# A chunked scan whose C Bᵀ products move forward in the order, a weighting done in one pass, and MLP products spread over four banks

## The reference, cut to what matters

```
cb      = C Bᵀ                              # 128 x 128 for each group
y_diag  = (cb * mask * decay * dt) x        # decay: 128 x 128 for each head
y_off   = (C h_prev) * exp(acs)
h       = chunk_decay * h_prev + Bᵀ(decay_to_end * dt * x)
y       = y_forward + y_backward + d_skip * x;   then y * SiLU(z)
```

## Time and profile before

| | us |
|---|---|
| median of 3 runs | 1688.41 (1687.32 to 1689.16) |
| profiled execution, its own time | 1688.6 |
| its span, first to last instruction | 1686.7 |
| PE busy | 1592.4 (94% of the span) |
| DVE busy | 1020.2 (60%) |
| ACT busy | 653.8 (39%) |

### The profile page before, as it was taken

How to read it: one execution, slowest core, us unless ns; L and a number is a source line. 1 busy time by engine, 2 the same in 40 slices (tenths; PEclk the granted TensorE clock), 3 DMA queues, 4 the chain that set the end, 5 groups by cost and what they waited for, 6 DMA issues and landing times.

```text
span 1686.7 us, 27239 instructions
## 1 busy us (share of the span) xinstructions
PE 1592.4 (94%) x11141; PEld 1503.7 (89%) x11141; DVE 1020.2 (60%) x1429; ACT 653.8 (39%) x1133; POOL 99.0 (6%) x155
## 2 busy tenths in 40 slices
PE   6999999989997998888899999999999999999997
PEld 2899999989997988888755699999989999999997
DVE  5777677738663677887566453436863353343468
ACT  3544444424463256675455533323521121121220
POOL 1001022100101100000000001000000000000000
PEclk9999999989998999999899999999999999999999
DMA  9545455432677666686440164335112222223221
GB/s 320 158 146 182 155 183 184 149 118 86 211 240 248 204 220 212 189 277 202 156 160 26 50 204 145 129 127 181 51 51 75 76 75 76 77 75 101 62 89 63
DMA packets 159895, 241.63 MB, mean 143 GB/s; under 512 B 8064, under 2 KB 126576, under 8 KB 156720
## 3 DMA queue, kind: packets, MB, share of 16 engines
q1 hardware_dynamic: 136608, 171.45, 31.2%
q0 software_dynamic: 12304, 47.72, 7.7%
q10 hardware_dynamic: 10880, 20.97, 4.6%
HBM read 195.06 MB, written 45.06 MB: 142 GB/s over the span
## 4 chain that ended last, share of the span: by engine, by line
PE 79%; DVE 10%; ACT 5%; issue 2%; DMA 2%; SPq 1%; ACTq 0%; DVEq 0%
PE acc L842 62%; PE tp L842 14%; ACT arena L1716 2%; PE tp L1257 1%; ACT whi L1472 1%; DVE arena L2272 1%; DVE wlo L1987 1%; PE tp L950 1%; DMA arena<-in_x_sample 1%; DVE arena L2274 1%; DMA y_nat<-arena 1%; DVE st L2005 1%; DMA raw<-in_w_in 1%; ACT whi L1853 1%; DVE wlo L2451 1%
## 5 line engine op out<-in xcount | busy, mean ns | idle before, releaser
L842 PE MATMUL acc<-hh,whi 128*128 128x322 f32 x1152 | 299.6, 321 | 13.3 <-issue 4.1
L842 PE MATMUL acc<-hl,whi 128*128 128x322 f32 x1152 | 294.5, 317 | 0.0
L842 PE MATMUL acc<-hh,wlo 128*128 128x322 f32 x1152 | 293.2, 315 | 0.0
L1987 DVE TENSOR_TENSOR wlo<-raw,whi 128x2048 fp32r<-128x2048 f32 x74 | 169.5, 2290 | 95.3 <-ACT whi L1472 95.3
L842 PEld LDWEIGHTS acc<-hh,whi 128*128 128x128 f32 x1152 | 204.6, 194 | 15.7 <-issue 4.5
L1472 ACT ACTIVATE whi<-raw 128x2048 fp32r<-128x2048 f32 x74 | 141.1, 1907 | 171.0 <-PE acc L842 166.9
L842 PEld LDWEIGHTS acc<-hl,whi 128*128 128x128 f32 x1152 | 205.9, 194 | 0.0
L842 PEld LDWEIGHTS acc<-hh,wlo 128*128 128x128 f32 x1152 | 205.7, 194 | 0.0
L842 PE MATMUL acc<-whi,hh 128*128 128x256 f32 x640 | 183.8, 287 | 0.0
L842 PE MATMUL acc<-whi,hl 128*128 128x256 f32 x640 | 180.6, 282 | 0.0
L842 PE MATMUL acc<-wlo,hh 128*128 128x256 f32 x640 | 180.4, 282 | 0.0
(11 more groups left out here) (296 smaller groups left out, 2909.8 us busy)
## 6 DMA issues: line engine op xcount, KB each, us to landing
raw<-in_w_in SPq DMA_DIRECT2D x38, 1024.0 KB, 6.9
raw<-in_w_mlp SPq DMA_DIRECT2D x32, 1024.0 KB, 5.4
arena<-in_w_mod SPq DMA_DIRECT2D x24, 1024.0 KB, 6.2
arena<-decay_sums_t ACTq DMA_DIRECT2D x40, 512.0 KB, 5.5
arena<-xs_nat SPq DMA_DIRECT2D x8, 1024.0 KB, 8.1
raw<-in_w_ssd_o SPq DMA_DIRECT2D x8, 1024.0 KB, 6.2
y_nat<-arena POOLq DMA_DIRECT2D x6, 1024.0 KB, 7.2
arena<-y_nat SPq DMA_DIRECT2D x6, 1024.0 KB, 6.5
```

The costliest lines, as they stand in the source:

```text
L842: return pe.matmul(out, l, r, start=first, stop=last)
L1987: dve.tensor_tensor(wlo[:, slot], raw[:, slot], whi[:, slot].bitcast(F32), ALU.subtract).then_inc(lo["sem"], step(lo))
```

## The change

It has five parts.

1. Preparation: five of the six filling pieces (before: two) stand ahead of `turn_h0(1)` on PE, and so on ACT ahead of `h0_out`; one (before: four) stands behind.
2. Latent chunks: PE's `products` stands behind the chunk's first piece; before it stood behind all three. ACT starts `exps` of group 0 ahead of the chunk's first piece, no longer behind it. On DVE, only in chunk 1, `masked` and `weighted(0)` stand ahead of two of its three first pieces.
3. `weighted` is one multiplication of 1024 columns instead of two of 512, and the addition as before.
4. `gated` of the quads 0 and 1 stands behind `weighted(4)` and `weighted(6)`, and that of quad 2 behind the last `combined`.
5. The MLP's second products go through the four banks acc 0 to 3.

```diff
@@ PE, preparation and scan
-            fill(2)
+            fill(F_H0 - 1)
             pe.wait_ge(s["h0_in"], 32)
...
             turn_h0(1)
-            fill(F_H0 - 2)
+            fill(1)
...
             for c in range(1, NT):
-                fill(F_LAT[c - 1])
+                fill(1)
                 if c == 1:
                     pe.wait_ge(bfree["sem"], value(bfree))
                     pe.wait_ge(h0c["sem"], value(h0c))
                 b = (c + 1) % 2
                 products(b)
+                fill(F_LAT[c - 1] - 1)
                 pe.wait_ge(bnin[b]["sem"], due(bnin[b]))
@@ PE, second_products
-                first_two([acc[:, 0, 0:BW], acc[:, 2, 0:BW]], (2, 2))
+
+                first_two([acc[:, 0, 0:BW], acc[:, 1, 0:BW]], (4, 4))
...
                         step(free)
-                        pe.wait_ge(free["sem"], value(free, 2))
-                        mlp_products(acc[:, 2 * ((NT * b + t) % 2), 0:BW], t, whi[:, b % 2], wlo[:, b % 2],
+                        pe.wait_ge(free["sem"], value(free, 4))
+                        mlp_products(acc[:, (NT * b + t) % 4, 0:BW], t, whi[:, b % 2], wlo[:, b % 2],
@@ ACT
-            weights(2)
+            weights(F_H0 - 1)
...
             h0_out(backs[0])
-            weights(F_H0 - 2)
+            weights(1)
...
             for c in range(1, NT):
+                exps(NG * c)
                 weights(1)
-                exps(NG * c)
                 if c > 1:
                     squares(c - 1, 2, zq[:, 0])
+                exps(NG * c + 1)
                 weights(1)
-                exps(NG * c + 1)
@@ DVE, weighted
-                for d in range(2):
-                    last = dve.tensor_tensor(ee[:, b, d], ee[:, b, d], cbm[:, d, g].unsqueeze(1).broadcast_to([P, R, P]), ALU.mult)
-                do(last)
+                do(dve.tensor_tensor(ee[:, b], ee[:, b], cbm[:, :, g].unsqueeze(2).broadcast_to([P, 2, R, P]), ALU.mult))
@@ DVE, a latent chunk
                 if c == 1:
-                    weights(F_LAT[c - 1])
+                    weights(1)
                 masked()
                 for g in range(NG):
                     weighted(g)
-                    weights(F_LAT_G[g] + (F_LAT[c - 1] if g == 0 and c > 1 else 0))
+                    if g in (4, 6):
+                        gated(c, g // 2 - 2)
+                    weights(F_LAT_G[g] + (F_LAT[c - 1] - (c == 1) if g == 0 else 0))
...
                         if q:
                             combined(y, q - 1, y[:, 8 * q - 8:8 * q])
-                            gated(c, q - 1)
                 combined(y, 3, y[:, 24:32])
+                gated(c, 2)
                 gated(c, 3)
@@ DVE, second_round
-                        dve.tensor_tensor(xo[:, t, cols], xo[:, t, cols], acc[:, 2 * ((NT * b + t) % 2), 0:BW],
+                        dve.tensor_tensor(xo[:, t, cols], xo[:, t, cols], acc[:, (NT * b + t) % 4, 0:BW],
```

## The result

The changed kernel takes 1691.67 us (median of 20 runs, 1687.49 to 1698.47); the kernel before takes 1688.45 us beside it (20 runs, 1684.01 to 1691.05). The ratio is 1.0021, with a 95% interval of 1.0011 to 1.0031: slower, by 3.2 to 3.6 us where 9.5 were forecast. The profiled execution took 1695.16 us (span 1693.2), that is 6.6 us over the profiled one of before and 3.5 us over its own kernel's median.

A forecast was written before the change was run, and what follows sets the result against it. PE, busy 94% of the span, was taken to bound the kernel, and the change to move its waits: 27.0 − 3.0 − 8.6 − 1.4 − 4.5 = +9.5 us on 1688.6, forecast 1698 us, range 1690 to 1704 (own case 1694 to 1703).

The forecast's parts named there:

- The mechanism: Three chunk turns: C Bᵀ waits 6.1 us for DVE's last `combined`, half clock follows, group 1's wait stays; 9.0 us each.
- the bank is free in time: Rival at the turns: DVE finishes its last `combined` before PE's one piece, turns cost 0; 1671 us, chance 0.05.
- the wait ahead of group 1 goes away: Rival at the turns: early C Bᵀ removes group 1's wait, a turn costs 2.9 us; 1679.6 us, chance 0.03.
- transfers in the preparation: Rival: a z block's store queues behind the backward state's, taking back up to 8.6 us; 1702 to 1707 us, chance 0.06.
- the clock recovers sooner or falls less often: Rival: new stalls lose 1.7 us or nothing, or shorter waits keep the clock up; 1690 to 1692 us, chance 0.08.
- The savings: Forecast gains: preparation 8.6 us, chunk 1 1.4 us, inside four chunks 3.0 us, MLP 4.5 us.
- the clock term of the sum: Behind the new wait at each of three turns: 5.8 us at half clock lose 2.9 us.
- the rest inside the chunks: Four chunks: one `gated` pass fewer ahead of `weighted(6)` and one-pass weighting shorten PE's waits, saving 3.0 us.
- MLP and all else behind the scan: MLP's second products: four banks remove three PE waits of 1.5 us for DVE's adds, saving 4.5 us.
- its terms: Part 2: three turns cost 27.0 us; earlier products start group 1 of chunk 1 sooner, saving 1.4 us.
- the bounds of the clock and of the merged pass: Half-clock loss of 1.7 us, or none, instead of 2.9 us a turn; merged weighting pass between 1.08 and 1.29 us.

The follow-up runs named there:

- e2: The changed kernel with C Bᵀ of chunks 2 to 4 behind two of the three first pieces instead of one: 1681.57 us, ratio 0.9966.
- e5: The changed kernel with part 2 taken back on PE, ACT and DVE, the rest of the change kept: 1672.71 us, ratio 0.9906.
- e3: The kernel before with PE's C Bᵀ behind the first piece and nothing else of the change: 1718.57 us, ratio 1.0178.
- e6: The kernel before with part 1, the preparation, alone: 1680.53 us, ratio 0.9958.
- e9: e5 with ACT's order of the change, while C Bᵀ stays behind three pieces: 1683.90 us, ratio 0.9974.
- e4: The changed kernel with 54 matmuls whose output nobody reads ahead of C Bᵀ in chunks 2 to 4: 1686.48 us, ratio 0.9992.
- e1: The changed kernel with C Bᵀ behind all three first pieces again, on PE alone: 1693.41 us, ratio 1.0027.
- e12: The kernel before with parts 3 and 4 alone, the one-pass weighting and the later gating: 1683.11 us, ratio 0.9979.
- e11: e8 with the filling piece of group 4 moved ahead of group 3: 1666.31 us, ratio 0.9872 against the kernel before.
- e8: e5 with `weighted(1)` ahead of the lower splits in chunks 1 to 4: 1664.81 us, ratio 0.9875 against the kernel before.

## Why the prediction was right in its sign and wrong in its size

**The mechanism held.** PE stands 6.3 us at each of three turns (6.1 forecast), the clock falls behind it, and group 1's wait stays. From the end of group 7 (705.80 + 0.83 = 706.63 in PE's timeline) to group 1 a turn takes 738.41 − 706.63 = 31.8 us, against 733.47 − 710.75 = 22.7 in the earlier trace rows: 9.1 us more where 9.0 were forecast. e2 shows that the wait is lack of cover and e5 that part 2 alone makes the change slower. The rivals "the bank is free in time", "the wait ahead of group 1 goes away" and "transfers in the preparation" fall with these rows. The remaining one, "the clock recovers sooner or falls less often", had a chance of 0.08 and the time that came (1690 to 1692 us). It has half of the mechanism: the new stalls did lose what I gave them, the old waits ahead of group 1 lost less.

**The savings held**: parts 1, 5 and 3 with 4 each by themselves, above. The wait of the preparation went, the store had landed; chunk 1's group 1 came at 608.17 instead of 618.26, 10.1 us sooner, 10.0 forecast (8.6 + 1.4).

**The step that failed is the clock term of the sum**: 2.9 us of new loss for each turn, 8.7 in three, with the loss behind the four waits ahead of group 1 left as it was. The length of the half clock behind a wait is not fixed by that wait. These are the times of the same 32 matmuls behind the waits ahead of group 1, from the chains (us; a dash where they are not on the chain):

| kernel | chunk 1 | 2 | 3 | 4 |
|---|---|---|---|---|
| before | 7.01 | 7.25 | 7.40 | 7.44 |
| changed | 6.27 | 6.27 | 6.29 | 6.29 |
| e2 | 6.28 | 7.44 | 7.83 | 7.66 |
| e3 | 6.83 | 7.70 | 7.59 | 7.57 |
| e6 | 6.77 | 6.28 | – | 6.87 |
| e9 | 6.24 | 7.37 | 6.25 | 7.49 |

```profile
750.84 7.59 PE acc L842 x32
667.27 6.28 PE acc L842 x32
```

The first row is e3's, some 21 us behind a new stall of 6.9 us: nothing is given back. The second is e6's, without any new stall and behind the same wait of 3.16 us as in the kernel before (7.25): 1.0 us is given back. So the changed kernel's gain behind group 1 is real in its profile, but it is not shown to come from the new stalls.

In the profiled executions the whole account is: preparation −8.8, chunk 1 −1.3, turns +27.2, behind the four waits ahead of group 1 −4.0, the rest inside the chunks −3.0 (−3.0 forecast), MLP and all else behind the scan −3.6 (−4.5 forecast, see the last section). That is +6.5, as from span to span. Of the 3.0 us that this is under the forecast, the 4.0 behind group 1 are more than all; the MLP takes 0.9 back.

**The other 3 us** lie between the profiled execution and the median. The profiled execution of the changed kernel is 3.5 us over its median, that of before 0.2 us over its own. Executions of one kernel differ by their mean granted clock: of the changed kernel 1687.49 us came with 0.981, 1695.16 with 0.974, 1698.47 with 0.973. I made the sum against one execution and took each of its half-clock stretches as owed. Which stretch the median execution lacks stays open, since only one execution of each kernel was profiled. But in medians, too, the miss lies in part 2 and not in the savings: part 2 costs 19.4 us, where its terms were 27.0 − 1.4 = 25.6. The stalls of 18.9 us less 1.4 are 17.5 of those 19.4, so the clock's part is 1.9 us (3.8 either way) where 8.7 were forecast. e4 has it at 5 us (2.4 either way), e3, where PE's order alone was changed, at 9.3 (3.0 either way). The price of the clock is thus anything from next to nothing to the full 8.7, by what else stands in the kernel.

In the stretch from 500 to 870 us, 48 us stand at half clock before (PEclk 0.95 over the first 100 us, 0.93 over the other 270) and 49 us after (1.00 and 0.91), within 3 us of rounding. The sum had 8.7 us of new loss against 2.0 us given back in the preparation, 6.7 net, which would be over 13 us more at half clock. The advice of the Trainium skill that I weighed (TensorE: Matmul & The Clock Gate, Why this matters for your kernels) is right in its direction, since e4 gains from keeping PE occupied; what it is worth was over-estimated by me, not by the page.

The prediction's range, too, has an end without a source: the bounds of the clock and of the merged pass give its 1694, but they put less than 1 us on top of 1698, and nothing there gives 1703.

**Open**: why one wait is followed by a longer time at half clock than another of the same length, or than the same wait in another kernel. No run here varied that by itself, and no kernel was profiled twice.

## What to carry to other kernels

A consumer moved ahead of the work that hides its producer costs that cover: two pieces of 3.6 us taken from ahead of C Bᵀ came back as a wait of 6.3 us. First lay the producer's own chain (the split, `carried`, `combined`) beside the pieces that cover it, and move the producer, not the consumer. Count stalls at full value, but count the clock as a range for the whole stage, from near nothing to the full loss behind each new stall, since here the loss behind old waits changed with every change of order; and make the sum against several executions' clocks. Orders on other engines that were changed together are undone together: half an undoing (e1) can cost as much as the change.

## What the runs showed of the hardware that was not expected

The same short wait is followed by a half clock in one execution and not in another. In the MLP PE waits 1.5 us before and 1.75 us after the change, at the same place of the program. PE's timeline and the stretch behind it, of the kernel before:

```profile
1448.45 0.56 PE L842 MATMUL acc<-hh,whi 128*128 128x322 f32 x2 [1.50 <-issue]
...
1448.50:1463.00 14.50, 14.50 (x98) 14.50 (x99) 4.84 (x4) 1.14 (x2) 0.00 (x0) 1.00 0.24 75
```

and of the changed kernel:

```profile
1455.23 0.56 PE L842 MATMUL acc<-hh,whi 128*128 128x322 f32 x2 [1.75 <-issue]
...
1456.30:1459.70 3.40, 3.40 (x16) 3.40 (x15) 1.45 (x1) 0.00 (x0) 0.00 (x0) 0.55 0.19 39
```

That half clock costs some 1.5 us (in the chain the 96 matmuls from 1455.23 on take 16.09 us, those of before from 1448.45 on 14.56). It does not belong to the four banks: e12, which has the MLP of before, shows it too (PEclk 0.58 from 1446.6 on, behind a wait of 1.90 us), and e9, which has the changed MLP, does not, behind a wait of 1.8 us. It may be one of the ways in which executions of one kernel come to differ by some us; that would need two profiles of one kernel.

A higher clock need not be time: e11's stretch from 600 to 870 us has a PEclk of 0.97 against 0.95 in e8, and by their ratios the two kernels take the same time. PE is busy for 237.4 of these 270 us in e11 and for 244.3 in e8: what the clock saves, it spends waiting.
